# Two transformer blocks in one kernel: the weight ring moves from the bottom of SBUF to the top

## The reference

```python
# first block
proj = rms_norm(h) @ w_in                       # q, k, v | conv inputs | z | gates
y_a  = moba_attention(rope(q_a), rope(k_a), v_a)          # 8 heads, causal
y_b  = rms_norm(gated_delta_rule(l2(q_b), l2(k_b), v_b, g, beta)) * silu(z)
h   += rms_norm((sig(gate_a) * (y_a @ w_proj_a) + sig(gate_b) * (y_b @ w_proj_b)) @ w_out)
f    = rms_norm(h)
h   += rms_norm((silu(f @ w_ffn_gate) * (f @ w_ffn_up)) @ w_ffn_down)    # 2816 wide
h   += sig(h @ w_ple_gate) * rms_norm(p @ w_ple)
# second block
proj = rmsnorm(x) @ w_in_2                      # q, k, v | pool input
mix  = concat([diff_attention(...), causal_multiscale_pool(u) @ w_pool]) @ w_out_2
x   += rmsnorm(mix)
x   += rmsnorm(cross_attention(rmsnorm(x) @ w_xq, mem_n @ w_xkv) @ w_xo)
x   += rmsnorm((silu(hf @ w_gate) * (hf @ w_up)) @ w_down)
```

## Time and profile before

| | us |
|---|---|
| median of the runs | 1046.01 |
| profiled execution | 1046.72 |
| its span, first to last instruction | 1044.7 |
| PE busy in it | 1002.7 |
| POOL (GpSimd) busy | 742.5 |
| ACT (ScalarE) busy | 527.5 |
| DVE (VectorE) busy | 381.5 |

### The profile page before, as it was taken

How to read it: one execution, slowest core, us unless ns; L and a number is a source line. 1 busy time by engine, 2 the same in 40 slices (tenths; PEclk the granted TensorE clock), 3 DMA queues, 4 the chain that set the end, 5 groups by cost and what they waited for, 6 DMA issues and landing times.

```text
span 1044.7 us, 14141 instructions
## 1 busy us (share of the span) xinstructions
PE 1002.7 (96%) x5396; PEld 850.1 (81%) x5396; DVE 381.5 (37%) x854; ACT 527.5 (50%) x775; POOL 742.5 (71%) x592
## 2 busy tenths in 40 slices
PE   5989999999999999999999999999999999999997
PEld 5978888988888877788888876789878868888885
DVE  4676432687532523412112343323262161111103
ACT  5474644455644434654545536566465355444431
POOL 6777542778442777789987777686958369999891
PEclk9999999999999999999999999999999999999999
DMA  8545231455231566477765555563636257766551
GB/s 267 180 128 179 81 102 61 122 163 182 99 102 61 172 193 202 146 217 215 205 195 165 161 172 190 204 211 106 199 118 205 64 159 218 206 188 194 169 174 40
DMA packets 76747, 167.51 MB, mean 160 GB/s; under 512 B 8348, under 2 KB 13704, under 8 KB 76552
## 3 DMA queue, kind: packets, MB, share of 16 engines
q1 hardware_dynamic: 71296, 156.40, 48.2%
q10 hardware_dynamic: 5384, 10.22, 3.0%
HBM read 165.55 MB, written 1.05 MB: 159 GB/s over the span
## 4 chain that ended last, share of the span: by engine, by line
PE 80%; DVE 6%; POOL 5%; ACT 5%; issue 2%; DMA 2%; DVEq 0%; ACTq 0%
PE L L473 19%; PE L L475 18%; PE L L474 18%; POOL w_lo L462 5%; PE Q L961 2%; PE Q L975 2%; PE L L842 2%; PE L L844 2%; PE L L843 2%; ACT w_hi L1170 2%; DVE small L1710 1%; DMA raw<-in_w_in 1%; PE Q L678 1%; PE Q L475 1%; PE Q L473 1%
## 5 line engine op out<-in xcount | busy, mean ns | idle before, releaser
L462 POOL TENSOR_TENSOR w_lo<-raw,w_hi 128x512 fp32r<-128x512 f32 x588 | 742.3, 1299 | 281.3 <-ACT w_hi L1170 280.6
L1170 ACT CAST w_hi<-raw 128x1024 fp32r<-128x1024 f32 x294 | 305.8, 1054 | 272.3 <-PE L L475 142.0
L473 PE MATMUL L<-w_hi,uH 128*128 128x512 f32 (+1 forms) x832 | 328.7, 395 | 13.2 <-POOL w_lo L462 4.8
L475 PE MATMUL L<-w_hi,uL 128*128 128x512 f32 (+1 forms) x832 | 319.2, 384 | 0.0
L474 PE MATMUL L<-w_lo,uH 128*128 128x512 f32 (+1 forms) x832 | 318.7, 383 | 0.0
L473 PEld LDWEIGHTS L<-w_hi,uH 128*128 128x128 f32 x832 | 157.1, 189 | 52.8 <-DVE uL L1741 10.3
L475 PEld LDWEIGHTS L<-w_hi,uL 128*128 128x128 f32 x832 | 156.9, 189 | 30.9
L474 PEld LDWEIGHTS L<-w_lo,uH 128*128 128x128 f32 x832 | 157.2, 189 | 27.6 <-issue 0.5
L473 PE MATMUL L<-w_hi,hH 128*128 128x512 f32 x176 | 70.3, 399 | 1.4 <-issue 1.4
L475 PE MATMUL L<-w_hi,hL 128*128 128x512 f32 x176 | 69.7, 396 | 0.0
L474 PE MATMUL L<-w_lo,hH 128*128 128x512 f32 x176 | 69.7, 396 | 0.0
(11 more groups left out here) (324 smaller groups left out, 1249.8 us busy)
## 6 DMA issues: line engine op xcount, KB each, us to landing
raw<-in_w_in SPq DMA_DIRECT2D x88, 512.0 KB, 3.6
raw<-in_w_ffn_gate SPq DMA_DIRECT2D x22, 512.0 KB, 3.7
raw<-in_w_ffn_up SPq DMA_DIRECT2D x22, 512.0 KB, 3.6
raw<-in_w_ffn_down SPq DMA_DIRECT2D x22, 512.0 KB, 3.5
raw<-in_w_gate SPq DMA_DIRECT2D x22, 512.0 KB, 4.3
raw<-in_w_up SPq DMA_DIRECT2D x22, 512.0 KB, 4.1
raw<-in_w_down SPq DMA_DIRECT2D x22, 512.0 KB, 3.5
raw<-in_w_out SPq DMA_DIRECT2D x16, 512.0 KB, 3.5
```

What stands on the lines that cost most here:

```text
L462: last = nc.gpsimd.tensor_tensor(w_lo[:, n % SPLIT, cc], raw[:, n % RAW, cc], w_hi[:, n % SPLIT, cc].bitcast(F32), ALU.subtract)
L473: mm(dst, sH, wH, start=start, stop=False)
L475: return mm(dst, sL, wH, start=False, stop=stop)
L1170: copy(w_hi[:, u % SPLIT, :], raw[:, u % RAW, :]).then_inc(w_hi_there, 1)
```

## The change

The three buffers of the ring are placed last and not first, and in another order: `w_hi`, `w_lo`, `raw` behind the 100 KB of the big area. Everything else is placed in the same order as before, from the same first free byte, and so lies 64 KB lower. Sizes, overlays and the distances between activations stay. Instructions, waits and their order are the same on every engine; line numbers behind the edit grow by one.

```diff
-        raw = place("raw", [P, RAW, UNIT])
-        w_hi = place("w_hi", [P, SPLIT, UNIT], F32R)
-        w_lo = place("w_lo", [P, SPLIT, UNIT], F32R)
         uH = place("uH", [P, KD, SEQ], F32R)
         uL = place("uL", [P, KD, SEQ], F32R)
         table = place("table", [P, 12 * P + 2 * NT * HD + ROPE2])
@@
         cpT = place("cpT", [P, NT, GH, SEQ], F32, Y)
-        used = B + 100 * KB
+        at[0] = B + 100 * KB
+        w_hi = place("w_hi", [P, SPLIT, UNIT], F32R)
+        w_lo = place("w_lo", [P, SPLIT, UNIT], F32R)
+        raw = place("raw", [P, RAW, UNIT])
+        used = at[0]
         assert used <= nc.sbuf_usable_end, (used, nc.sbuf_usable_end)
```

## The result

| | before | after |
|---|---|---|
| median of 7 runs | 1046.87 | 1049.17 |
| lowest and highest | 1044.28 to 1048.28 | 1048.82 to 1050.65 |
| profiled execution, its span | 1046.72, 1044.7 | 1049.08, 1047.1 |

After takes 1.0029 times as long as before, with the interval [1.0017, 1.0040]: slower by 1.8 to 4.2 us. The forecast was 1054, 8 us slower. The direction came, and so did the mechanism of the large term; more than half of the size did not.

What follows compares the result with a forecast made beforehand. The prediction took the rate at which TensorE's matmuls start one behind the other as the bound; +10.5 (`u` weights), -0.5 (256 columns), -1.7 (conv) and 0 (both odd) gave +8.3 us, so 1054, range 1047 to 1058.5.

Steps and rivals of the forecast that it cites:

- the large term: 2304 matmuls of 512 columns with `uH`/`uL` weights: 226.7 to 233.4 ns each, 12.8 us, +10.5 on the path.
- no settling: Sign: 512-column `w_hi`,`uH` steps at 0.2336 us from the first step, also behind an interruption.
- The one in six: Share of the 2304 steps estimated to pay the slower rate already, behind interruptions; lowers 15.4 to 12.8 us.
- the share of 0.82: Part of the split-product matmul time (569 of 691 us) taken to lie on the path; scales step changes.
- The 192 at 256 columns: 256-column matmuls with `uH`/`uL` weights turn mixed (one start 32 past a multiple of 64): -3.3 ns each, -0.5 us.
- The conv: Its 576 matmuls turn to even stream, odd weights (32 past a multiple of 64): -3.3 ns each, -1.7 us on the path.
- 0.456 ns a column for every mixed pairing: Matmul rate claimed whenever one operand starts at a multiple of 64 and the other 32 past, whichever it is.
- the 720 and 192 that turn from mixed to both odd: 512-column `h`, `y`, `m` weights and streamed `mH`, `mL`; both starts become 32 past a multiple of 64: taken as 0.
- both-odd settles: Rival, chance 0.31: pairs both 32 past a multiple of 64 settle like even/even, -3.4 us, total 1050.9.
- The ports: Trainium skill's objection: separate read ports for streamed operand and weights, so the ring's place changes nothing, 1046.
- Only the weights' place counts: Rival, chance 0.10: the 2304 keep 226.7 ns, the conv gains 1.7 us at most; 1044.3 to 1046.
- An odd stream is better in itself: Rival, chance 0.11: streams from the ring, 32 past a multiple of 64, run faster; -8.6 us, total 1037.4.

Runs made afterwards that it cites:

- e2: Kernel before with the ring left at the bottom but 32 bytes higher and everything behind it 64 bytes higher: 1054.23 us, 1.0069 times before.
- e5: Kernel before, ring at the bottom, with `table` and `small` placed last, so every ring matmul pair has distance 0 modulo 256: 1043.47 us, 0.9961 times before.
- m1: Program of matmuls alone, without the two blocks, 40 per setting, one start moved: 512 columns 226.7 ns at distance 0, 233.3 at 32 bytes.
- e1: Changed kernel with the ring 32 bytes higher, its starts again multiples of 64: 1047.37 us, 1.0007 times before.
- e4: Kernel before with 32 bytes added ahead of `raw` and again ahead of `Y`, all starts but `small` 32 past a multiple of 64: 1047.06 us, 1.000 times before.

## Why the prediction was right and wrong

- **The path.** Right: matmul starts set the pace, the other engines, casts and transfers kept their times, and `u` weights went from 0.2267 to 0.2336. Behind an interruption the steps of after are at 230 to 235 ns from the first on, with no settling, as forecast. The first three are those of before as well (232, 230 and 232 ns in the mean); only from the fourth on do the two kernels part.
- **The large term, 12.8 us of steps and 10.5 on the path.** Right in size, and in part by luck: 11.5 at the matmuls, less 0.8 in waits in their place and 0.4 in waits behind them, is 10.3. Two errors cancel in that. The one in six that already paid came out at 1 - 11.5 / 15.4, one in four: before needs about nine steps to settle, not five. And the share of 0.82 took 2.3 us for lost where these waits gave back 1.2.
- **The 192 at 256 columns, -0.5.** Measured -0.5.
- **The conv, -1.7.** Half of it: -0.9. The step fell from 0.1200 to 0.1181, not to 0.1169. "0.456 ns a column for every mixed pairing" was read from one distance at 512 columns (224) and from 32 at 256 columns, with 224 there only for weights of 16 columns; it is no law of both.
- **The step that failed: the 720 and 192 that turn from mixed to both odd, taken at 0.** Measured -4.4 and +0.6, together -3.8, while its bound was -3.4. (The -4.4 is of 744 matmuls: the sum left out 24 with `pH`, `pL` weights, -0.2 of it. The bound was -4.2 at the matmuls, and the down steps gained 1.7 us each, nothing of it lost on the path.) It is the rival "both-odd settles", held at 0.31, that came true. The reason given for the 0, that every stream that is not even/even shows the mixed rate, was no evidence: before has no odd/odd stream of this kind, so the trace could not show one settling. The argument named beside the rival, the same offset of one operand to the other, was the cause; e2, e5 and m1 show it.
- **Why the rule looked right.** In before and after the remainder by 64 and the distance go together: even/even and odd/odd are the pairings at D = 0. e1 to e4 pull them apart.
- **The total.** With the clock alike in both executions the terms make 10.3 - 0.5 - 0.9 - 3.8 = 5.1. Another 1.1 us went between full float32 matmuls, 4.0 in all. The forecast had nothing there, and their steps did not change; the 1.0 us lies in five waits, and such waits move by 0.46 from one execution of before to the other. Whether the change shortened them is not shown. The profile of after lacks the clock's fall as well, and shows 2.1. The 7 runs of each give 3.0. Executions of the same mean granted clock give more: at 0.998 before takes 1045.4 in the mean of ten executions (all runs of before taken together) and after 1049.1 in the mean of five, 3.7 apart; at 0.996 it is 1047.3 (eleven) and 1050.6 (two), 3.4 apart. How often the clock fell in a set of runs is therefore a part of its median.
- **The ports.** The Trainium skill, "SBUF — State Buffer", section "Who interferes with whom", gives PE's streamed operand and its weights read ports of their own. By that no row of m1's table should differ from another, and at 512 columns they differ by 3%. The measurement decides for this format; for bfloat16 and full float32 m1 agrees with the page at the few distances tried.
- **The rivals that fell.** "Only the weights' place counts": after kept the weights' remainder for `uH`, and the step moved. "An odd stream is better in itself": the steps went up.

## What to carry to other kernels

When a change moves buffers and no instruction, list for each matmul the distance from the weights' start to the streamed start modulo 256 bytes, not the alignment of either. In the short float32 format put streams of 512 columns at a multiple of 256 bytes from their weights; streams of 256 columns want another distance (192 was best). 128 and 384 columns and the other two formats showed no difference between 0 and 32; other distances should be measured before one relies on that. A small odd-sized table between two groups of tiles is enough to spoil it, and placing it last cost nothing here and gave 0.33 to 0.39%.

An equal total proves no rule: e1 matched before to 0.07% with other steps in it. Read the step of each kind, and where the trace has no row of a pairing, give its two bounds like chances rather than 0 to one of them.

## What the runs showed of the hardware that was not expected

The step of a matmul in the short float32 format depends on the distance of its two operands in SBUF with a period of 256 bytes, by up to 3% at 512 columns (226.7 to 234.3 ns; 236.7 at 240 bytes) and 6% at 256 (113.3 to 120.0), and the best distance of one width, 0, is with 96 the worst of the other. It follows neither start by itself, and neither bfloat16 nor full float32 shows it between 0 and 32 bytes. What in the engine makes it is open; no run tells. The fast step of 256 columns at D = 192 shows in the two blocks too: e1's conv went at 113.6 ns and gained 2.9 us. But the conv streams the same `uH` that is the weights of the 512-column products, so that its 192 is their 64, and they lost 3.4. One place of `w_hi` does not serve both.

TensorE's granted clock fell to its lower level at the same 3.5 us of the program in some executions of a kernel and not in others, and in two of twelve profiles a second time at 703 us. Each fall cost 1.5 us.
